# A Trainium2 encoder-layer kernel: row gathers spread over the selection, one low half moved ahead, two GELU loads moved back

## The reference

```python
q = (xt @ wq).reshape(T, PEER_HEADS, 2, PEER_HALF)
s = jnp.einsum('thpd,hpnd->thpn', q, subkeys)
sv, si = lax.top_k(s, K)                      # 16 of 128 keys, two sides
comb = (sv[:, :, 0, :, None] + sv[:, :, 1, None, :]).reshape(T, PEER_HEADS, K * K)
cs, ci = lax.top_k(comb, K)
idx = ia * PEER_NKEYS + ib                    # the chosen experts
g = jax.nn.softmax(cs, axis=-1)
a = jnp.einsum('td,thkd->thk', xb, u_tab[eb])
w = gb * jax.nn.gelu(a)
out = jnp.einsum('thk,thkd->td', w, v_tab[eb])
```

## Time and profile before

| | us |
|---|---|
| median of 3 runs (1307.8 to 1309.76) | 1308.54 |
| the profiled execution | 1311.27 |
| its span, first to last instruction | 1309.5 |
| TensorE busy in the span | 1277.6 |
| VectorE busy | 1135.1 |
| ScalarE busy | 684.8 |
| GpSimd busy | 695.0 |

### The profile page before, as it was taken

The page is one execution under the profiler, slowest core; times in us unless marked ns, Lnnn a source line. Parts: engine busy times, 40 slices in busy tenths (PEclk is TensorE's granted clock), DMA queues, the critical chain, the costliest instruction groups (busy, mean ns, idle before and its releaser), DMA issues.

```text
span 1309.5 us, 22032 instructions
## 1 busy us (share of the span) xinstructions
PE 1277.6 (98%) x7713; PEld 714.9 (55%) x7713; DVE 1135.1 (87%) x2414; ACT 684.8 (52%) x962; POOL 695.0 (53%) x407
## 2 busy tenths in 40 slices
PE   6999999999999899999999999999999999999997
PEld 3554555545666677777765555555444444444444
DVE  8865488897999898988968889899898998989997
ACT  5652655457566788888844433434333343433342
POOL 3741233357775476676634656567674555545502
PEclk9999999999999999999999999999999999999999
DMA  7222422238999699999999999999999999999951
GB/s 303 98 97 81 129 81 81 97 121 302 323 327 360 212 396 421 392 400 396 406 397 399 359 371 365 374 377 414 397 388 406 406 405 403 406 406 404 405 203 65
DMA packets 115224, 404.92 MB, mean 309 GB/s; under 512 B 10832, under 2 KB 46800, under 8 KB 99536
## 3 DMA queue, kind: packets, MB, share of 16 engines
q1 hardware_dynamic: 73680, 253.07, 51.2%
q0 software_dynamic: 41472, 151.01, 29.8%
HBM read 358.96 MB, written 44.56 MB: 308 GB/s over the span
## 4 chain that ended last, share of the span: by engine, by line
PE 69%; DVE 17%; issue 7%; ACT 2%; DMA 2%; POOL 1%; DVEq 0%; SPq 0%; ACTq 0%; POOLq 0%
PE bank L822 32%; PE bank L810 9%; PE bank L812 9%; PE bank L811 9%; PE bank L1087 2%; DVE area L1763 2%; DVE area L1754 2%; DVE area L1756 2%; DMA raw<-tiles_dram 2%; PE bank L837 2%; PE bank L1029 2%; PE bank L1031 2%; DVE area L1760 1%; DVE area L1751 1%; DVE ple_gate L2017 1%
## 5 line engine op out<-in xcount | busy, mean ns | idle before, releaser
L822 PE MATMUL bank<-cut,area 128*128 128x512 f16 x2208 | 482.0, 379 | 2.2 <-DVE cut L1517 2.2
L810 PE MATMUL bank<-hT,cut 128*128 128x352 f16 (+1 forms) x1216 | 393.6, 324 | 7.6 <-POOL cut L672 5.7
L811 PE MATMUL bank<-hT,cut 128*128 128x352 f16 (+1 forms) x1216 | 393.5, 324 | 0.0
L812 PE MATMUL bank<-hT,cut 128*128 128x352 f16 (+1 forms) x1216 | 393.5, 324 | 0.0
L822 PEld LDWEIGHTS bank<-cut,area 128*128 128x128 f16 x2208 | 215.9, 98 | 259.2 <-DVE cut L1517 3.4
L1517 DVE SCALAR_TENSOR_TENSOR cut<-raw,cut 128x1024 f16<-128x1024 f32 x214 | 269.8, 1262 | 66.8 <-ACT cut L1125 41.8
L1125 ACT ACTIVATE cut<-raw 128x1024 f16<-128x1024 f32 x214 | 221.9, 1049 | 194.7 <-DMA raw<-tiles_dram 157.6
L672 POOL TENSOR_TENSOR cut<-raw,cut 128x1024 f16<-128x1024 f32 x76 | 161.8, 2138 | 171.4 <-DVE window_word L1769 83.8
L810 PEld LDWEIGHTS bank<-hT,cut 128*128 128x128 f16 x1216 | 119.2, 98 | 84.0 <-issue 4.0
L812 PEld LDWEIGHTS bank<-hT,cut 128*128 128x128 f16 x1216 | 119.2, 98 | 75.6
L811 PEld LDWEIGHTS bank<-hT,cut 128*128 128x128 f16 x1216 | 119.2, 98 | 74.4 <-issue 0.3
(11 more groups left out here) (226 smaller groups left out, 1598.5 us busy)
## 6 DMA issues: line engine op xcount, KB each, us to landing
raw<-tiles_dram SPq DMA_DIRECT2D x105, 1024.0 KB, 13.1
raw<-tiles_dram SPq DMA_DIRECT2D x88, 512.0 KB, 3.7
gates_scratch<-area SPq DMA_DIRECT2D x12, 2048.0 KB, 9.5
area<-gates_scratch SPq DMA_DIRECT2D x31, 768.0 KB, 15.8
gelu_scratch<-gelu_out SPq DMA_DIRECT2D x88, 192.0 KB, 5.1
area<-gelu_scratch SPq DMA_DIRECT2D x22, 768.0 KB, 16.8
norm_rows<-norms_dram SPq DMA_DIRECT2D x3, 1024.0 KB, 6.8
hn<-x_dram SPq DMA_DIRECT2D x4, 512.0 KB, 5.1
```

Source lines behind the costliest of these rows:

```text
L810: nc.tensor.matmul(dst, w[0], hT[:, 0, k, 0:width], start=(k == 0), stop=False)
L811: nc.tensor.matmul(dst, w[0], hT[:, 1, k, 0:width], start=False, stop=False)
L812: last = nc.tensor.matmul(dst, w[1], hT[:, 0, k, 0:width], start=False, stop=(k == KD - 1))
L822: mm = nc.tensor.matmul(bank[:, 2 * tt + h, :], lhs(a)[:, tt * P:(tt + 1) * P], cut[:, t.slot, b, h * HALF:(h + 1) * HALF], start=(first a ...
```

## The change

Four edits. In the selection, a table `GATHERED` says how many of the first 32 gathers have gone out by the end of each window, in place of a rule that sent as many as the row slots allow; the first four of window 12 go out behind its third low half. At the gate rounds, GpSimd issues two gathers fewer ahead of the first low half, then two behind each. On VectorE the first softmax low half comes ahead of the transpose and the gate bias, the second between the two bias adds. On SP the loads of GELU groups 0 and 1 stand behind pairs p = 3 and 5 of the last `both`, where they stood behind 1 and 3.

```diff
+GATHERED = {12: 8, 13: 14, 14: 18, 15: 22, 16: 27, 17: 32}
...
-                    if e == EIGHTS - 1 and p in (1, 3):
+                    if e == EIGHTS - 1 and p in (3, 5):
                         sp.wait_ge(sparse_w_done, 1)
-                        load_gelu(p // 2)
+                        load_gelu(p // 2 - 1)
...
-                if n > 2 * LATTER_HALF + 1:
-                    for _ in range(begun, min(EARLY, dotted + EARLY_SLOTS)):
-                        gather(begun)
-                        begun += 1
+                    if n == 2 * LATTER_HALF + 2 and j == 2:
+                        for _ in range(begun, GATHERED[n]):
+                            gather(begun)
+                            begun += 1
+                for _ in range(begun, GATHERED.get(n, begun)):
+                    gather(begun)
+                    begun += 1
...
-            for n in range(EARLY, EARLY + ROW_RING):
+            for n in range(EARLY, EARLY + ROW_RING - 2):
...
-                for n in range(EARLY + ROW_RING + (SOFT_DOTS + 2 * pair if pair else 0), EARLY + ROW_RING + SOFT_DOTS + 2 * pair + 2):
+                for n in range(EARLY + ROW_RING - 2 + 2 * pair, EARLY + ROW_RING + 2 * pair):
                     gather(n)
-            for n in range(EARLY + ROW_RING + SOFT_DOTS + U_GATES, EXTRA + 2 * HK):
+            for n in range(EARLY + ROW_RING - 2 + U_GATES, EXTRA + 2 * HK):
...
+            dve.wait_ge(lo_cut, POOL_FIRST + POOL_TILES)
+            split_lo(softmax_tiles[0])
             dve.wait_ge(rows_used, EXTRA)
...
             add_gate_b(0)
+            split_lo(softmax_tiles[1])
             add_gate_b(1)
-            dve.wait_ge(lo_cut, POOL_FIRST + POOL_TILES)
-            split_lo(softmax_tiles[0])
-            split_lo(softmax_tiles[1])
```

More of the change, by code:

```diff
@@ L1877, in _ @@
                 top_k(unit, *where)
+            softmax_tiles = [Tile(T_U + U_TOPK + SPLIT_AHEAD + j) for j in range(U_SOFTMAX)]
+            dve.wait_ge(lo_cut, POOL_FIRST + POOL_TILES)
+            split_lo(softmax_tiles[0])
             dve.wait_ge(rows_used, EXTRA)
@@ L1886, in add_gate_b @@
                 nc.vector.tensor_tensor(gate_t, gate_t, gate_b_row, ALU.add).then_inc(gate_biased, 1)
-            softmax_tiles = [Tile(T_U + U_TOPK + SPLIT_AHEAD + j) for j in range(U_SOFTMAX)]
             add_gate_b(0)
+            split_lo(softmax_tiles[1])
             add_gate_b(1)
-            dve.wait_ge(lo_cut, POOL_FIRST + POOL_TILES)
-            split_lo(softmax_tiles[0])
-            split_lo(softmax_tiles[1])
             dve.wait_ge(gate_exp, 1)
```

## The result

The changed kernel is slower: 1312.75 us median of 22 runs (1307.63 to 1316.08) against 1309.3 for 22 runs of before (1307.31 to 1312.86). The ratio is 1.0024, 95% interval 1.0016 to 1.0032, so 3.1 us slower. The prediction was 1307.1, range 1302.4 to 1309.6.

What follows compares the result with a forecast made beforehand. The prediction took TensorE, busy nearly all the time, as the bound, its waits limiting any gain. A front gain of 5.75 us and a GELU-load cost of 4.35 gave -1.4, from 1308.54 to 1307.1 us, range 1302.4 to 1309.6.

Steps and rivals of the forecast that it cites:

- the one on the gate rounds: Gate rounds: fewer gathers ahead of the low halves win 2.9 us; the shorter row ring costs nothing.
- The selection: Windows' gathers: 4.51 us won at U tile 10, but VectorE's lead spent waiting for rows in window 17.
- The stall at U tile 10: Selection: TensorE's wait for GpSimd goes, 2.66 us of wait and 1.85 of clock, together 4.51 us.
- the new wait of 1.9 us at U tile 32: Selection, window 18: TensorE, ahead of VectorE, would wait 1.9 us for GpSimd's low half.
- The front's 5.75: Selection to gate rounds: total gain taken as 5.75 us, between bounds of 5.2 and 8.8.
- The softmax low half: Behind the selection's last dot: first softmax low half ends at 413.5 instead of 416.46; next one's lead shrinks to 2.3 us.
- The GELU loads: Late pair: group 1 ahead of it delays landing 3.1 us; with the clock, 4.35 us slower.
- The clock: Late pair: a TensorE stand of 4.7 us, over 2.66, lowers the clock and adds 1.85 us.
- rival 1: Late pair: the GELU load is hidden, only the front part counts, 1302.8 us; chance 0.2.
- rival 2: Late pair: the longer stand does not drop the clock, 1305.8 us; chance 0.13.
- Rival 3: Selection: VectorE keeps much of its lead, GELU load still costs 4.35, 1304.1 us; chance 0.1.
- Rival 4: Window 18: a late row makes TensorE stand 4.0 us and drops the clock, 1311.0 us; chance 0.09.

Runs made afterwards that it cites:

- the filled ring: Changed kernel with the four rows held back by the gate rounds sent one more in each of pairs 1 to 4: 0.9975 of before.
- the run that holds the rows back: Changed kernel with the ring left four rows short behind the gate rounds too, filling by one row for every five: 0.9982 of before.
- old rounds kernel: Changed kernel with the gathers of the gate rounds as they were before, the other edits kept: 0.9995 of before.

## Why the prediction was wrong

**The step that failed** is the one on the gate rounds: "The row ring runs two pairs ahead of its dot instead of four ... I cost it at nothing". I looked only at whether a row still lands before its own dot. It does. I did not ask when the four rows that the rounds hold back are sent. They go behind the last round in one burst, onto DMA engines that are full, beside two gate loads and a raw pair that had 5 us to spare. In place of -2.9 us the edit measured +2.5 alone. In the changed kernel it cost 3.8 (1.0024 against 0.9995), and there its two halves are +6.4 for the burst by the filled ring, 5.5 by the run that holds the rows back, and -2.6 for the low halves. The same error is in the sentence "TensorE has no wait between 480 and 940": true of before, and used as if it held after. A stretch without a wait can be 5 us from one, and what tells it is the landing of each pair beside its use, which I read for the late pair alone. With +2.5 in place of -2.9 my sum is -2.85 + 2.5 + 4.35 = +4.0, near the measured 3.1.

**The selection**: right in what it wins, and wrong in what it gives back. The stall at U tile 10 and the low clock behind it are gone, 4.49 us at U tile 31 against 4.51. VectorE waited for rows in window 17, 2.37 and 0.61 us, where I had said 2 or more. But VectorE kept 2.2 us of lead where I gave it none (window 18's low halves began at 400.71 instead of 402.94), so the new wait of 1.9 us at U tile 32 did not come: 0.2 us for GpSimd in all. The front's 5.75 less 2.9 for the rounds is 2.85, and 3.4 was measured.

**The softmax low half**: right in what it does (it ended at 411.7 where I had 413.5, and 1.16 us of stand stayed), and a condition of the selection's gain that I had not stated: without it that gain is lost at U tile 34.

**The GELU loads**: size right, 4.35 against 4.6, 4.5, 4.1 and 2.8, cause wrong, so the size is in part luck. I had 3.1 us of landing from the load's place in the queue, a landing over 24 us and a stand of 4 to 5. The changed kernel's pair landed after 21.9 us, 0.6 more than before, and TensorE stood 2.68. In the profiles of the six kernels with the new places the pair landed 20.3 to 23.9 us after its issue, 22.3 on average; in the seven with the old places 18.5 to 22.4, 20.2 on average. That is 2.1 us, and it was 24.0 where no GELU load stood between the gate loads in front of it. What makes the rest is not settled. An estimate from the mean granted clock of all runs of a kernel gives the clock 1.6 us of the 4.6 (0.9964 with the loads moved, 0.9976 before) and 1.8 of the 4.5 (0.9954, 0.9968), but 0.1 of the 4.1 (0.9981, 0.9982). In that last pair of profiles TensorE's stands at the late pair are 4.23 and 0.83 us, 3.4 more, and TensorE comes to the pair 0.8 us earlier where the loads are moved.

**The clock**: I took a stand of over 2.66 us as enough to lower it. It is likely, not certain, and the price can be twice mine (last section).

**The rivals**: rival 1 is out, since the loads cost 4.6 us alone. What rival 2 says of the clock happened in the profile with the GELU loads alone (3.15 us of stand, no fall) and not in that of the changed kernel. Rival 3 was half right in VectorE's lead, 2.2 us of 4.8, and wrong in the total. Rival 4 needed a stand in window 18 that did not come. The case that happened, slower through a stand elsewhere, was not among them. The median of before also came out 0.8 us higher with 22 runs than the 1308.54 I had started from; this does not touch the ratio.

## What to carry to other kernels

When a prefetch ring is made shorter in a loop, ask where the difference is sent, not only whether each item is still in time; if it is behind the loop, it goes as a burst, and what it hits is the next load that another queue issues. Where DMA engines are full, a load moved later may leave a hole that nothing fills; here kernels with a moved load and such a hole were 3 to 5 us slower than the same kernels without, though the hole as the cause is argued only. So look at the rates of both places. And an earlier TensorE is only worth what the next low half, tile or weight is early: windows and softmax low half were worth nothing apart and 3.4 us together.

## What was not expected of the hardware

The clock's fall is not a function of the stand alone. With the ring filled TensorE stood 3.63 us in the profiled execution, and the window in which it started again and those behind show a granted clock of 1.00:

```profile
937.00:938.00 1.00, 0.08 (x1) 0.09 (x2) 1.00 (x2) 0.49 (x2) 0.00 (x0) 1.00 1.02 418
938.00:939.00 1.00, 1.00 (x5) 0.42 (x6) 1.00 (x1) 0.57 (x1) 0.00 (x0) 1.00 1.04 424
```

With both loads behind p = 3 it stood 4.29 us at the same place, and the clock was at its lower level, 0.50, in all windows from 938 to 943:

```profile
938.00:939.00 1.00, 0.43 (x2) 0.15 (x3) 1.00 (x2) 0.15 (x1) 0.00 (x0) 0.50 1.03 420
...
942.00:943.00 1.00, 1.00 (x4) 0.41 (x3) 1.00 (x2) 1.00 (x2) 0.78 (x1) 0.50 0.69 168
```

Stands of 3.15 and 3.63 us passed without a fall in a profile, and one of 2.18 us (gate rounds, old rounds kernel, at 448) had one behind it, as had 2.18 us with the softmax low half alone; with the kernel before the same 2.18 us had none.

Nor is the price of a fall always the same. Between 300 and 1000 us the seventeen profiles of this case hold twenty falls. What the clock misses of 1.00 in its windows of 1 us adds up to 1.7 us in sixteen of them and to 3.4 us in four (behind stands of 2.97, 3.50, 4.29 and 4.50 us). The longest stand, 4.67 us with the rows held back, cost 1.7.

Executions of one kernel differ in this way: of the twelve runs with the ring filled, seven had a mean clock of 0.999 and took 1304.6 us on average, two had 0.996 and took 1308.7. By an estimate, 0.003 of 1304 us, 3.9 of these 4.1 us are the clock. The Trainium skill ("TensorE: Matmul & The Clock Gate", Part 1) says that the chip looks at activity in windows that run freely and do not start with the kernel; that the same 2.18 us lower the clock in one profile and not in another agrees with it, but no run here shows the windows. For a forecast it means that the clock's price belongs in with a chance, and that one profile does not show whether a stand pays it.
